# Three products with a second network's modulation weights are moved into the feed-forward stages of the first

## The reference, cut to what matters

```
def adaln_params(cvec, w, b):
    return jnp.split(jax.nn.silu(cvec) @ w + b, 6, axis=-1)

for i in range(DEPTH):                     # second network
    sh1x, sc1x, g1x, sh2x, sc2x, g2x = adaln_params(c, ada_w[i], ada_b[i])
    sh1c, sc1c, g1c, sh2c, sc2c, g2c = adaln_params(c_ctx, ada_w[i], ada_b[i])
    hx = rmsnorm_2(x, norm_g[i, 0]) * (1.0 + sc1x) + sh1x
    # layer 0: x += g1x * fourier_mix(hx);  layer 1: x += g1x * rwkv(hx, hc)
    # then both: x += g2x * ec_moe(rmsnorm_2(x, norm_g[i, 1]) * (1.0 + sc2x) + sh2x)
```

## Time and profile before

| | |
|---|---|
| time, median of 3 runs | 2977.51 us |
| lowest and highest | 2976.88, 2978.76 us |
| span of the profiled execution | 2971.2 us |
| PE, DVE, ACT busy, share of the span | 91%, 40%, 33% |
| mean DMA rate, bytes moved | 238 GB/s, 707.05 MB |
| loads of the ring (1 MB each) | 624 |

### The profile page before, as it was taken

The page is one execution under the profiler, slowest core; times in us unless marked ns, Lnnn a source line. Parts: engine busy times, 40 slices in busy tenths (PEclk is TensorE's granted clock), DMA queues, the critical chain, the costliest instruction groups (busy, mean ns, idle before and its releaser), DMA issues.

```text
span 2971.2 us, 56865 instructions
## 1 busy us (share of the span) xinstructions
PE 2703.1 (91%) x24486; PEld 1793.9 (60%) x24486; DVE 1199.3 (40%) x1792; ACT 984.4 (33%) x1704; POOL 192.3 (6%) x200
## 2 busy tenths in 40 slices
PE   8999999999999999999999989899999989866676
PEld 6877777878877778885433323344787764432332
DVE  4545566545456566543100101423677763000001
ACT  4445545434445555531110000202455542000000
POOL 0002000000002000000000000002333310000000
PEclk9999999999999999999999999999999999978777
DMA  6474234574573345533899999941100028999998
GB/s 257 175 292 154 103 138 179 185 292 179 191 285 117 122 166 213 178 127 137 354 421 421 421 421 421 393 177 56 57 11 17 11 78 330 421 420 421 418 420 337
DMA packets 101397, 707.05 MB, mean 238 GB/s; under 512 B 11780, under 2 KB 12548, under 8 KB 18224
## 3 DMA queue, kind: packets, MB, share of 16 engines
q1 hardware_dynamic: 90864, 657.17, 56.2%
q10 hardware_dynamic: 9648, 43.91, 3.8%
q0 software_dynamic: 656, 2.52, 0.2%
HBM read 702.47 MB, written 1.07 MB: 237 GB/s over the span
## 4 chain that ended last, share of the span: by engine, by line
PE 65%; DMA 20%; DVE 8%; ACT 6%; issue 2%; SPq 0%; ACTq 0%; DVEq 0%
DMA weight_ring<-in_stream 20%; PE banks L2040 9%; PE banks L650 8%; PE banks L652 7%; PE banks L651 7%; PE banks L1870 3%; PE banks L2405 3%; PE banks L1017 3%; PE banks L1019 2%; PE banks L1018 2%; PE banks L2451 2%; ACT front L1281 1%; PE banks L1177 1%; PE banks L2847 1%; PE banks L1931 1%
## 5 line engine op out<-in xcount | busy, mean ns | idle before, releaser
L2040 PE MATMUL banks<-weight_ring,scratch 128*32 128x256 f32 (+1 forms) x4304 | 566.1, 507 | 148.9 <-DMA weight_ring<-in_stream 147.3
L2040 PEld LDWEIGHTS banks<-weight_ring,scratch 128*32 128x32 f32 (+1 forms) x4304 | 186.0, 129 | 509.1 <-DMA weight_ring<-in_stream 261.1
L647 DVE TENSOR_TENSOR split_high<-weight_ring,split_high 128x1024 fp32r<-128x1024 f32 x198 | 242.2, 1230 | 256.0 <-ACT split_high L642 255.3
L642 ACT CAST split_high<-weight_ring 128x1024 fp32r<-128x1024 f32 x198 | 206.9, 1052 | 287.8 <-PE banks L652 223.9
L2191 DVE TENSOR_TENSOR scratch<-scratch,banks 128x512 f32<-128x512 f32 (+1 forms) x32 | 17.8, 555 | 570.4 <-PE banks L2040 570.4
L1369 DVE TENSOR_TENSOR split_high<-weight_ring,split_high 128x1024 fp32r<-128x1024 f32 x128 | 161.5, 1272 | 159.6 <-ACT split_high L1266 159.6
L650 PE MATMUL banks<-split_high,features_low 128*128 128x512 f32 x480 | 189.8, 395 | 0.0
L1266 ACT CAST split_high<-weight_ring 128x1024 fp32r<-128x1024 f32 x128 | 133.4, 1049 | 164.5 <-PE banks L1019 158.5
L652 PE MATMUL banks<-split_high,features_high 128*128 128x512 f32 x480 | 187.1, 390 | 0.0
L651 PE MATMUL banks<-split_high,features_high 128*128 128x512 f32 x480 | 186.8, 389 | 0.0
L2100 ACT ACTIVATE scratch<-banks 128x512 f32<-128x512 f32 (+1 forms) x32 | 15.7, 491 | 471.6 <-PE banks L2040 471.6
(11 more groups left out here) (438 smaller groups left out, 4693.9 us busy)
## 6 DMA issues: line engine op xcount, KB each, us to landing
weight_ring<-in_stream SPq DMA_DIRECT2D x624, 1024.0 KB, 10.6
scratch<-in_kept ACTq DMA_DIRECT2D x20, 1024.0 KB, 10.2
scratch<-in_pair_rows ACTq DMA_DIRECT2D x8, 448.0 KB, 3.7
scratch<-in_kept ACTq DMA_DIRECT2D x6, 512.0 KB, 5.9
scratch<-in_lora ACTq DMA_DIRECT2D x2, 1536.0 KB, 17.6
front<-in_gain_rows ACTq DMA_DIRECT2D x5, 512.0 KB, 3.7
bias<-bias_rows POOLq DMA_DIRECT2D x1, 2304.0 KB, 15.0
scratch<-in_routing ACTq DMA_DIRECT2D x1, 1040.5 KB, 5.0
```

The costliest lines, as they stand in the source:

```text
L642: act.copy(split[i % 4][0], source(i)).then_inc(*self.rounded.up())
L647: dve.tensor_tensor(lo, source(i), hi.bitcast(F32), ALU.subtract).then_inc(*self.rest.up())
L2040: last = pe.matmul(self.psum[q * M:(q + 1) * M, (GATE, UP, DOWN)[part], 0:W], left, w[j][:, q * W:(q + 1) * W], start=(k == 0), stop=(k == ...
```

## The change: what it does

The product `silu(c) @ w` of a group is made in another way and in another place. In each of the four feed-forward stages, on the way up, groups 1 to 8 get a third chunk, of the modulation weights, between their two own chunks. DVE (`weigh`) multiplies the chunk, 128 x 2048, by one column of silu(c) (a value per partition) and adds it to running sums of the same shape. After 8 chunks PE (`add_up`) sums over the 128 partitions with four matmuls whose stationary operand picks one row of 32; DVE saves the 128 x 512 result. A chunk of this kind is released by PE together with the group's last chunk (`both_done`). The sums are of one stream only, so group 0, which needs both, is made twice: groups 1, 0, 2 for the tokens and group 0 for the context take the four stages. The three `ada_chunk` runs in the RWKV part are gone, and there DVE takes the saved rows. The stream has 32 such chunks where it had 24: 632 loads of the ring in place of 624.

Beside this, the loads for a table of attention biases at the program's start move from POOL's queue to ACT's, and the write and read back of that table to SP's, between the first six loads of the ring and the others. POOL then issues no transfers, and memory set aside for them is given up.

```
 def chunk_of(i):
     pair = i // 2
-    return c0 + pair + (min(max(pair - 2 * groups, 0) // 4 * 4, KT) if ada is not None else 0)
+    return c0 + pair + min((pair - 1) // 2 if pair else 0, KT) + (min(max(pair - 2 * groups, 0) // 4 * 4, KT) if ada is not None else 0)
...
+        def follows_weighted(i):
+            return i % 4 == 3 and 7 <= i < 7 + 4 * KT
+        def both_done(ins):
+            self.chunks_used.count += 2
+            ins.then_inc(self.chunks_used.sem, 2)
+        def weigh(dve, k):
+            self.wait_chunk(dve, chunk_of(4 * k + 7) - 1)
+            if k == 0 and with_bias:
+                dve.wait_ge(self.early["conditioned"].sem, 1)
+            c, w = self.ada[:, 32 * k + stream:32 * k + stream + 1], self.slot(chunk_of(4 * k + 7) - 1)
+            if k == 0:
+                ins = dve.tensor_scalar(self.partial_sums[:, :], w, c, None, ALU.mult)
+            else:
+                dve.wait_ge(self.weighted.sem, weighted0 + k)
+                ins = dve.scalar_tensor_tensor(out=self.partial_sums[:, :], in0=w, scalar=c, in1=self.partial_sums[:, :], op0=ALU.mult, op1=ALU.add)
+            ins.then_inc(*self.weighted.up())
+        def add_up(pe):
+            pe.wait_ge(self.weighted.sem, weighted0 + KT)
+            for j in range(4):
+                last = pe.matmul(self.psum[32 * j:32 * j + 32, 7, :], self.pick[:, 1 - stream:33 - stream],
+                                 self.partial_sums[:, j * NB:(j + 1) * NB], start=True, stop=True)
+            last.then_inc(*self.added_up.up())
...
-                    for t in range(TT):
-                        last = up(n, i, t)
-                    half_done(last, i)
+                    last = up(n, i, 0)
+                    if follows_weighted(i):
+                        pe.wait_ge(self.weighted.sem, weighted0 + n)
+                    last = up(n, i, 1)
+                    if follows_weighted(i):
+                        both_done(last)
+                    else:
+                        half_done(last, i)
...
+                if i == UP + 2 * KT - 1:
+                    add_up(pe)
...
                 for i in range(4 * n + 4, 4 * n + 8):
                     rest_half(dve, i)
+                if n < KT:
+                    weigh(dve, n)
...
+                if i == N - 2:
+                    dve.wait_ge(self.added_up.sem, added0 + 1)
+                    saved = self.second_mod[:, group * NB:(group + 1) * NB]
+                    if stream:
+                        dve.tensor_tensor(saved, saved, self.psum[:, 7, :], ALU.add).then_inc(*ve.up())
+                    else:
+                        dve.tensor_copy(saved, self.psum[:, 7, :]).then_inc(*ve.up())
...
             rows_ready(pe, 2)
-            modulation(a0, 4)
             turn(0, 6)
...
             wait(pe, self.parts_high, 4)
-            modulation(g0, 7)
             pe.wait_ge(self.params_loaded.sem, params)
             low_rank(0, xj, T4, 4, 4)
...
-            def modulation(g, bank, end, bias, n):
-                dve.wait_ge(self.chunks_used.sem, end)
-                dve.tensor_tensor(mod[:, g, :], self.psum[:, bank, :], bias, ALU.add).then_inc(*mods["aff_ready"].up())
+            def modulation(g, bias):
+                dve.tensor_tensor(mod[:, g, :], self.second_mod[:, g * NB:(g + 1) * NB], bias, ALU.add).then_inc(*mods["aff_ready"].up())
...
             for s in range(RING):
                 sp.dma_start(self.slot(s), stream[s]).then_inc(self.slot_loaded[s], 16)
+            self.mirror(sp)
```

More of the change, by code:

```diff
@@ L594, in seam, with ffn @@
         return on_act, on_dve, turn
-    def ffn(self, stage, ada=None, inner=None):
+    def ffn(self, stage, second, ada=None, inner=None):
         nc, ve = self.nc, self.ve
@@ L2366, in _ @@
         def _(pe):
-            def modulation(chunk, bank):
-                for k in range(KT):
-                    self.ada_chunk(pe, chunk + k, k, self.silu_c, bank)
             def turn_mod(g, bank, n):
@@ L2928, in y_state @@
                     ins.then_inc(*y_ready.up())
-            def modulation(s, k):
-                if s == units + 1 and k == 0:
-                    pe.wait_ge(lr_masked.sem, units)
-                self.ada_chunk(pe, self.chunk + k, k, self.silu_c, F[0])
             def output_gates():
@@ L3547, in _ @@
             turn(pe, 0)
-        self.chunk += KT
         @self.block.scalar
@@ L3690, in _stream, with up @@
     ada = [_ada(i["ada_w_2"][l])[KT * g:KT * (g + 1)] for l in range(DEPTH) for g in range(3)]
+    def up(w, group):
+        for n, chunk in enumerate(_gate_up(w)):
+            parts.append(chunk[None])
+            if n % 2 == 0 and 2 <= n < 2 + 2 * KT:
+                parts.append(ada[group][n // 2 - 1:n // 2])
     def down(w, group=None):
@@ L3750, in layout @@
     second = N_CHUNKS - MOE_CHUNKS
-    first = second - MOE_CHUNKS - 3 * KT - 16
+    first = second - MOE_CHUNKS - 16
     kept = [start + at for start, places in zip((first, second), KEPT_AT) for at in places]
```

86 lines of the change are left out of this document (39 added, 47 removed).

## The result

| | before | after |
|---|---|---|
| median | 2978.11 us of 4 runs (2976.88 to 2978.76) | 2958.66 us of 4 runs (2955.77 to 2961.18) |
| ratio, 95% interval | | 0.9938 (0.9925 to 0.9952) |
| profiled execution: span | 2971.2 us | 2956.0 us |
| profiled execution: its own time | not on record; about 2973.0 us (experiment 1) | 2957.75 us |
| instructions | 56865 | 56637 |

The kernel is faster by 0.6%. The forecast was 2957.7 us, 19.8 us less than before. The medians are 19.5 apart, the ratio with its interval stands for 14 to 22 us, and the two profiled executions are 15.2 apart. Since single executions of one program differ by more than 10 us, the total cannot say which terms of the sum were right. What follows finds that out.

The account below looks back on a forecast made before the run. Expert runs wait for weights; elsewhere the chain of waits, largely through PE, counts. Terms -8.9 - 11.0 - 3.5 + 3.6 = -19.8 us take the median 2977.51 to 2957.7 us; own range 2954 to 2963, four-fifths range 2951 to 2967.

Parts of the forecast that it names:

- four `add_up`: Feed-forward stages: four added sums of 0.9 us each on PE's path cost 3.6 us in all.
- first run: RWKV part's start, group 0: without its chunks the modulation is turned 8.9 us earlier; bounds 6 and 10.
- second run: Group 2, between first projection and low-rank products: its place closes up, saving 11.0 us; lower bound 8.
- scan, eight pieces: Scan's last steps: removing four matmul pieces on the chain saves 3.5 us, bounds 2 and 4; four hidden ones give nothing.
- the first rival: First projection: PE idles more, its clock drops, costing 1.3 up to 4 us (2959 to 2962); chance 0.12.
- Third run: Group 1 in the scan's last steps: four pieces totalling 4.0 us on the chain, taken as 3.5 saved.
- more than forecast: Scan: a 2.84 us gap beside a burst of loads goes too if the burst caused it, 2953 to 2955; chance 0.09.
- The clock: Rival at the projection: removed matmuls kept PE's clock up, so 1.3 to 4 us go back; chance 0.12.
- Added work: Feed-forward stages: four sums cost 3.6 us; 32 DVE weighings of 2.2 to 2.6 us and the extra ring chunks are hidden.
- The slower rival: Feed-forward groups on the way up: the released chunk pair lands too late and PE waits, 3006 us; chance 0.06.
- Outside the span: Whole run: 6.3 us outside the profiled span were added to the predicted span of 2951.4, giving 2957.7 us.

Follow-up runs that it names:

- experiment 1: The kernel before with only the bias loads moved to other queues and the smaller reserved DMA scratch: 2976.14 us against 2975.46, ratio 0.9999.
- middle_filler: The changed kernel with 32 matmuls of the removed form put back between first projection and low-rank product, no chunks streamed: 2963.54 us, ratio to before 0.9963.
- experiment 8: The changed kernel with five pieces of four matmuls, without chunks, in the scan's last two steps and ahead of the output: 2957.47 us, ratio to before 0.9942.
- scan_filler: The changed kernel with 32 matmuls put back at the eight old places in the scan's last two steps, no chunks streamed: ratio to before 0.9942.
- tail_warm: The kernel of experiment 8, the changed one with five added matmul pieces around the scan's end: 2957.47 us, ratio to before 0.9942.
- before_loads_late: The kernel before with ScalarE's three late scan loads (1.31 MB) issued later, after the fifth state copy of the second-last step: 2980.42 us, ratio 1.0012.

## Why the prediction was right, and where its sum was not

| part | forecast | measured, profile to profile | measured, all profiles |
|---|---|---|---|
| four `add_up`, up to the RWKV part | +3.6 | +2.6 | +4.9 |
| first run | -8.9 | -8.3 | -8.3 to -8.7 |
| second run | -11.0 | -9.8 | -9.8 to -14.3 |
| scan, eight pieces | -3.5 | -0.9 | -0.9 to +2.7 |
| scan, up to its last two steps | 0 | 0.0 | -0.6, in means |
| from the output projection to the end | 0 | +1.3 | +0.2, in means |
| sum of the spans | -19.8 | -15.2 | |

The last column uses the stretches that the experiments left as they were: eight profiles of the changed kernel's way to the RWKV part against four of the old one's (mean start of L1998 at 1888.4 and 1883.5 us), all of the starts and middles that were not edited, and for the last two steps the five of equal scan against 50.00 (in means 50.6 against 50.0 for the three old kernels with the loads in place). Taken in means throughout, the last column adds up to -14.8 us.

*First run.* Right, and for the reason given: the turning waits for DVE alone, and the 7 us of matmuls weigh nothing. Counted from the gates' rows, the modulation is turned 8.8 us earlier (1898.41 against 1904.64), as worked out, and the projection 8.3.

*Second run.* Right in mechanism. The place closed up; in this profile 1.3 of the 11.0 went to the projection's colder clock, 30.75 us in place of 29.43, which is the first rival's sum. But from the projection to low_rank the changed kernels take from 27.6 to 30.6 us with the same code, and the clock orders them: with a granted clock of 1.00 in the projection's first 8 us it is 27.6 us, with 0.79 to 0.82 it is 29.0 to 29.3, with 0.68 30.1 and with 0.62 or 0.63 30.5 to 30.6. The four old kernels all have 0.79 to 0.81. So the colder start in this profile is one draw of several, not a fixed price of the change.

*Third run.* This step failed: "Four pieces on the chain, 1.00 + 0.99 + 1.00 + 0.99 = 4.0 us ... I take 3.5". The pieces were on the chain, and the last four were hidden, as the text had it. What I left out are two things that pay the gain back. The first is TensorE's clock. Without the pieces, the rest of the scan's end takes 28.1 to 29.2 us in five kernels against 27.3 in three old ones, 0.8 to 1.9 more; in the last ten us before the output projection the granted clock is 0.66 in middle_filler and 1.00 in the kernel before. The clock at the step's beginning is not decided by the pieces alone (experiment 8). The second is the stop beside the pieces, which did not go. Its rival "more than forecast" had asked whether the burst was its cause. The stop goes with the burst, but the burst had two parts, ring loads and ScalarE's three, and the change removes one. In the changed kernel the stop is 1.47 to 4.30 us, for a reason that no run shows. With the three loads moved in both kernels the pieces, their ring loads and the stop together were worth 7.2 us. The step that failed is thus the overlap: 3.5 us held for free standing pieces, and what was removed also carried the clock, while what made the stop stayed.

*The clock* was given 0.12 as a rival that replaces the forecast. It was no alternative to it but a part of every run. One more place: behind the fourth feed-forward stage the first expert's 64 matmuls (L1985) take 7.4 us in two of the changed kernels and 8.7 to 9.2 in the other six with that code, against 7.8 in all four of the old. This is after, then scan_filler:

```profile
1425.63 7.38 PE L1985 MATMUL banks<-scratch 128*128 128x128 f32 x64 [0.28 <-DVE scratch L2227]
```

```profile
1426.52 9.11 PE L1985 MATMUL banks<-scratch 128*128 128x128 f32 x64
```

with a granted clock from 1424 to 1436 of 1.00 and 0.74. Ahead of them lies a wait of 2.9 us for DVE in either.

The Trainium skill, "TensorE: Matmul & The Clock Gate" (Part 1), says that an idle engine falls to half of its clock and is brought back by sustained work. The trace agrees in part: in the changed kernel the clock fell near 2416, after a stop of 1.47 us that ended at 2413.86, and was 0.50, the level of 1.2 GHz, from 2420 to 2426, against 0.99 in scan_filler, where pieces had gone ahead. In tail_warm it stayed at 0.50 up to the last `gw`, with PE busy 5.68 of the six us before it.

*Added work.* The sums at 0.97 to 1.0 us each, the weighing at 2.35 us (1.28 for the first of each stage, which has nothing to add to) hidden up to twice its size, the ring at 277 GB/s without a late chunk: all close to the forecast. The slower rival, a pair of chunks that comes too late, did not occur in any of 44 groups. What the way to the RWKV part takes beyond four sums, 4.9 us in means, lies in part in the expert matmuls above.

*Outside the span.* The 6.3 us were an error of bookkeeping, but they cancel: 2951.4 + 6.3 is 2977.51 - 19.8. As the span of the profiled execution, 2951.4 was 4.6 too low, since the gain between the two profiles is 15.2.

*The number.* It came out within 1 us, and that is luck. Against the means the first two terms were off by 0.5 and 0.2 us, but the four sums by 1.3 and the scan by 4.0. By ratios (0.9938 to 0.9944 for the changed kernel and the variants that cost nothing) the gain is 17 to 18.5 us, by the stretches in means 14.8, by the two medians 19.5. The forecast of 19.8 lies above all of these, inside the interval of the ratio. Its own range of 2954 to 2963 is not the sum of its bounds either: these give 2956 (10 + 11 + 4 - 3.6) to 2965.

## What to carry to other kernels

Before pricing work that is to be removed from a chain, put it back elsewhere as an empty copy: the same eight pieces cost 0.0 us at one place and 7.0 at the other. Where a product is removed between short waits, look at the granted clock behind it, in more than one execution, since the pieces may have been paying for their successors and the clock differs between executions of equal code. And set a profile's span against the time of that same execution, not against a median.

## What the runs showed of the hardware

- In the changed kernel and its variants PE stops with the releaser "issue" for 1.5 to 4.3 us while or just after a burst of 1.31 MB fills the DMA engines in the scan; with the burst split in three or moved the longest stop was 0.9 to 1.2 us. In before_loads_late a ring load of 1 MB alone went with a stop of 2.85.
- The same projection code took 27.6 us with a granted clock of 1.00 in its first 8 us and 30.6 with 0.62, in different executions of equal code.
- Four float32 matmuls of 128x32 by 128x512 into four groups of 32 partitions lasted as long as one (1.06 and 1.05 us).
- DVE operations beside GpSimd's 128x1024 additions were stretched from 0.17 to 2.16 us and from 1.09 to 3.17 us, the reduction L3199 beside them not at all (1.07). The Trainium skill, "SBUF — State Buffer" (SBUF: two separate sides), says that GpSimd and those operations of DVE that read two SBUF inputs or run in a two-port mode hold one pair of ports in turn. L3206 has two such inputs and L3199 one, so the trace agrees for these. L3200 has one; no row shows whether it runs in such a mode, but a TENSOR_SCALAR of 128x2048 in SBUF (L678) takes 1283 ns where the two-input L681 takes 2346.
